# Moving the LayerNorm steps of the last two tiles to other places in the stream, and passing the last LayerNorm between the engines in four pieces

## The reference, cut to what matters

```python
mix = concat([attn, c], axis=-1) @ w_out            # attention and a LayerNormed, SiLUed convolution ("cln")
h = layer_norm(ALPHA * x + mix, ln1_g, ln1_b)       # "ln1"
up = h @ w_up
upc = causal_dwconv(concat([ffn_prev, up]), ffn_dw_w, ffn_dw_b)
f = (silu(upc[..., :2816]) * upc[..., 2816:]) @ w_down
ple = sigmoid(h @ w_pg + b_pg) * (p @ w_pe)
y = layer_norm(ALPHA * h + f + ple, ln2_g, ln2_b)   # "ln2", the output
```

## Time and profile before

| | us |
|---|---|
| median of 3 runs | 2485.96 (2484.69 to 2487.77) |
| the profiled execution, its own time | 2489.22 |
| its span, first to last instruction | 2487.4 |
| PE busy | 2393.0 (96%) |
| POOL busy | 1606.6 (65%) |
| DVE busy | 1449.9 (58%) |
| ACT busy | 1277.6 (51%) |
| mean granted PE clock | 0.982 |

### The profile page before, as it was taken

How to read it: one execution, slowest core, us unless ns; L and a number is a source line. 1 busy time by engine, 2 the same in 40 slices (tenths; PEclk the granted TensorE clock), 3 DMA queues, 4 the chain that set the end, 5 groups by cost and what they waited for, 6 DMA issues and landing times.

```text
span 2487.4 us, 38824 instructions
## 1 busy us (share of the span) xinstructions
PE 2393.0 (96%) x15109; PEld 2351.9 (95%) x15109; DVE 1449.9 (58%) x2338; ACT 1277.6 (51%) x2070; POOL 1606.6 (65%) x1284
## 2 busy tenths in 40 slices
PE   7789999999999999999999999999999999998996
PEld 7789998999999999999999999999899999988996
DVE  5747884467666357666626767652676665264432
ACT  4547555466444446644445654453565435355652
POOL 7447787775665676566567656656865655667773
PEclk9889999999999999999999999999999999999998
DMA  6324454543333444333344433334443332534442
GB/s 226 102 96 153 152 184 152 177 145 117 113 125 115 160 155 144 119 117 127 104 164 155 146 122 115 124 109 162 154 148 109 125 134 97 169 118 165 167 147 79
DMA packets 119046, 341.54 MB, mean 137 GB/s; under 512 B 15312, under 2 KB 43600, under 8 KB 118864
## 3 DMA queue, kind: packets, MB, share of 16 engines
q1 hardware_dynamic: 95408, 311.32, 37.2%
q10 hardware_dynamic: 23456, 27.74, 3.4%
HBM read 330.12 MB, written 8.99 MB: 136 GB/s over the span
## 4 chain that ended last, share of the span: by engine, by line
PE 85%; DVE 6%; ACT 4%; issue 2%; POOL 1%; DMA 1%; ACTq 0%; SPq 0%; DVEq 0%
PE ps L511 27%; PE ps L513 27%; PE ps L512 27%; DVE sq L1116 2%; POOL w_lo L462 1%; PE ps L602 1%; DMA w_raw<-in_panels 1%; ACT w_hi L630 1%; PE ps L550 1%; DVE acc L1053 1%; PE ps L581 1%; PE ps L569 1%; PE ps L559 1%; DVE res L1053 1%; DVE ps L1156 0%
## 5 line engine op out<-in xcount | busy, mean ns | idle before, releaser
L462 POOL TENSOR_TENSOR w_lo<-w_raw,w_hi 128x512 fp32r<-128x512 f32 (+1 forms) x1272 | 1605.6, 1289 | 842.3 <-ACT w_hi L630 840.8
L630 ACT CAST w_hi<-w_raw 128x1024 fp32r<-128x1024 f32 (+1 forms) x636 | 622.2, 981 | 605.9 <-PE ps L513 418.6
L511 PE MATMUL ps<-h_hi,w_hi 128*128 128x386 f32 (+5 forms) x2496 | 816.0, 327 | 9.6 <-DVE f_lo L994 4.1
L512 PE MATMUL ps<-h_lo,w_hi 128*128 128x386 f32 (+5 forms) x2496 | 807.6, 324 | 0.0
L513 PE MATMUL ps<-h_hi,w_lo 128*128 128x386 f32 (+5 forms) x2496 | 807.6, 324 | 0.0
L511 PEld LDWEIGHTS ps<-h_hi,w_hi 128*128 128x128 f32 x2496 | 473.6, 190 | 18.2 <-issue 9.4
L512 PEld LDWEIGHTS ps<-h_lo,w_hi 128*128 128x128 f32 x2496 | 474.3, 190 | 1.3
L513 PEld LDWEIGHTS ps<-h_hi,w_lo 128*128 128x128 f32 x2496 | 474.6, 190 | 0.0
L511 PE MATMUL ps<-f_hi,w_hi 128*128 128x384 f32 (+2 forms) x1264 | 412.0, 326 | 10.1 <-DVE f_lo L994 5.5
L512 PE MATMUL ps<-f_lo,w_hi 128*128 128x384 f32 (+2 forms) x1264 | 407.6, 322 | 0.0
L513 PE MATMUL ps<-f_hi,w_lo 128*128 128x384 f32 (+2 forms) x1264 | 407.5, 322 | 0.0
(11 more groups left out here) (128 smaller groups left out, 2025.2 us busy)
## 6 DMA issues: line engine op xcount, KB each, us to landing
w_raw<-in_panels SPq DMA_DIRECT2D x540, 512.0 KB, 3.2
w_raw<-in_panels SPq DMA_DIRECT2D x48, 384.0 KB, 3.0
w_raw<-in_panels SPq DMA_DIRECT2D x48, 128.0 KB, 2.3
xres<-in_xT ACTq DMA_DIRECT2D x32, 192.0 KB, 2.9
out_yT<-res ACTq DMA_DIRECT2D x4, 1536.0 KB, 6.5
a_raw<-in_xT ACTq DMA_DIRECT2D x6, 768.0 KB, 6.7
out_yT<-res ACTq DMA_DIRECT2D x2, 1024.0 KB, 4.9
x_raw<-in_xT SPq DMA_DIRECT2D x1, 1536.0 KB, 7.3
```

Of the source, the lines that this page charges most:

```text
L462: ins = pool.tensor_tensor(w_lo[:, n % WS, c], w_raw[:, n % RS, c], w_hi[:, n % WS, c].bitcast(F32), ALU.subtract)
L511: pe.matmul(out, w_hi[:, sl, c], hi, start=k == 0, stop=False)
L512: pe.matmul(out, w_hi[:, sl, c], lo, start=False, stop=False)
L630: act.copy(w_hi[:, n % WS, 0:w], w_raw[:, n % RS, 0:w]).then_inc(w_hi_done, 1)
```

## The change

Five things. (1) The cast `h_hi` of ln1 and of cln is a step of its own, `high`. For tiles 1 to 4 it stands one group later (n = 13), with `lo` at 14; for tile 0 one group later too. (2) In tile 4 the steps of ln2 of tile 3 stand later: `tree` 12 (was 11), `mean` and `centre` 15 (13), `square` 16 (14), `sqtree` 18 (16), `var`, `root`, `scale` 20 (18, 18, 19), `affine` 21 as before. (3) ln1 of tile 5 is no longer in `DIRECT`: it gets the two DVE trees, and its steps stand at n = 1, 3, 4, 5, 7. (4) The tree of ln2 of tile 4 stands at n = 7, ahead of the first `u` group, and its other steps at slots 0, 1, 2, 4, 5 (they were at 2, 2, 3, 5, 6, the tree at 0). (5) ln2 of tile 5, the last of the program, gets code of its own: PE adds block m-1 to the mean behind `d` group m, DVE subtracts, ACT squares and DVE scales in four pieces of two blocks each with a semaphore count per piece, the affine is done for blocks 0 to 4 on ACT and 5 to 7 on DVE, and SP sends the output in two halves, four DMAs where ACT sent two.

The core of the diff:

```diff
             one = {2: ("mean", "centre"), 3: ("square",), 6: ("sqtree",), 9: ("var", "root"), 10: ("scale",),
-                   12: ("affine",), 13: ("lo",)}
+                   12: ("affine",), 13: ("high",), 14: ("lo",)}
...
+            if i == LAST - 1:
+                two = {12: ("tree",), 15: ("mean", "centre"), 16: ("square",), 18: ("sqtree",), 20: ("var", "root", "scale"),
+                       21: ("affine",)}
         elif i:
-            one = {0: ("mean", "centre", "square"), 3: ("var", "root", "scale", "affine", "lo")}
-            two = {}
+            one = {1: ("mean", "centre", "square"), 3: ("sqtree",), 4: ("var", "root", "scale"), 5: ("affine", "high"),
+                   7: ("lo",)}
+            two = {7: ("tree",)}
...
-        late = {0: ("tree",), 2: ("mean", "centre", "square"), 3: ("sqtree",), 5: ("var", "root", "scale"), 6: ("affine",)}
+        late = {0: ("mean", "centre"), 1: ("square",), 2: ("sqtree",), 4: ("var", "root", "scale"), 5: ("affine",)}
...
     for m in range(KB):
         stage("d", LAST, 2, m)
-    for name in ("tree", "mean", "centre", "square", "sqtree", "var", "root", "scale", "affine"):
-        stage(name, "ln2", LAST)
+        if m:
+            stage("last_mean", m - 1)
+    stage("last_mean", KB - 1)
+    stage("tree", "ln2", LAST)
+    stage("last_norm")
...
-DIRECT = (("cln", 0), ("ln1", 0), ("ln1", LAST), ("ln2", LAST))
+DIRECT = (("cln", 0), ("ln1", 0))
...
+            y = O["yT"].rearrange("(b p) t -> p b t", p=P)
+            for half in range(2):
+                b = slice(HB * half, HB * half + HB)
+                sp.wait_ge(end_act, LAST_ACT if half else HB)
+                if half:
+                    sp.wait_ge(end_dve, KB - LAST_ACT)
+                for tok, c, cnt in prompt_and_sample(LAST, STARTS[LAST], SEQ):
+                    sp.dma_start(y[:, b, c:c + cnt], res[:, b, tok:tok + cnt]).then_inc(y_out, 16)
...
+            def last_mean(m):
...
+                pe.wait_ge(down_done, (LAST * 3 + 2) * KB + m + 1)
+                mm = pe.matmul(ps[:, AUX, 0:w], mean8[:], res[:, m, 0:w], start=m == 0, stop=m == KB - 1)
...
+            def last_variance():
...
+                for k in range(KB):
+                    if k % 2 == 0:
+                        pe.wait_ge(sq_done, END + k // 2 + 1)
+                    mm = pe.matmul(ps[:, AUX + 1, 0:w], mean8[:], sq[:, k, 0:w], start=k == 0, stop=k == KB - 1)
...
+            def last_norm():
...
+                for n, b in enumerate(PIECES):
+                    act.wait_ge(centred, END + n + 1)
+                    act.activation(sq[:, b, 0:w], res[:, b, 0:w], ACT.Square).then_inc(sq_done, 1)
+                load_functions(ACT.Sqrt)
...
+                for k in range(LAST_ACT):
...
+                    act.wait_ge(scaled, END + k // 2 + 1)
...
+            def last_norm():
...
+                for b in PIECES:
+                    z = res[:, b, 0:w]
+                    dve.tensor_tensor(z, z, std.unsqueeze(1).broadcast_to([P, 2, w]), ALU.mult).then_inc(scaled, 1)
+                dve.wait_ge(scaled, END + len(PIECES))
+                for k in range(LAST_ACT, KB):
+                    r = res[:, k, 0:w]
+                    dve.tensor_scalar(r, r, prm("ln2_g", k), prm("ln2_b", k), ALU.mult, ALU.add).then_inc(end_dve, 1)
```

More of the change, by code:

```diff
@@ L95, in mix_at @@
         for name, n in (("tree", 25), ("mean", 26), ("centre", 26), ("square", 27), ("sqtree", 28), ("var", 29),
-                        ("root", 29), ("scale", 30), ("affine", 31), ("lo", 32)):
+                        ("root", 29), ("scale", 30), ("affine", 31), ("high", 31), ("lo", 32)):
             if k == n:
@@ L137, in plan @@
     stage("conv_add", 0, 3)
-    for name in ("tree", "mean", "centre", "square", "sqtree", "var", "root", "scale", "affine", "lo"):
+    for name in ("tree", "mean", "centre", "square", "sqtree", "var", "root", "scale", "affine", "high", "lo"):
         stage(name, "cln", 0)
@@ L150, in plan @@
             one = {2: ("mean", "centre"), 3: ("square",), 6: ("sqtree",), 9: ("var", "root"), 10: ("scale",),
-                   12: ("affine",), 13: ("lo",)}
+                   12: ("affine",), 13: ("high",), 14: ("lo",)}
             two = {11: ("tree",), 13: ("mean", "centre"), 14: ("square",), 16: ("sqtree",), 18: ("var", "root"),
                    19: ("scale",), 21: ("affine",)}
+            if i == LAST - 1:
+                two = {12: ("tree",), 15: ("mean", "centre"), 16: ("square",), 18: ("sqtree",), 20: ("var", "root", "scale"),
+                       21: ("affine",)}
         elif i:
-            one = {0: ("mean", "centre", "square"), 3: ("var", "root", "scale", "affine", "lo")}
-            two = {}
+            one = {1: ("mean", "centre", "square"), 3: ("sqtree",), 4: ("var", "root", "scale"), 5: ("affine", "high"),
+                   7: ("lo",)}
+            two = {7: ("tree",)}
         else:
-            one = {0: ("mean", "centre", "square"), 2: ("var", "root", "scale"), 4: ("affine",), 5: ("lo",)}
+            one = {0: ("mean", "centre", "square"), 2: ("var", "root", "scale"), 4: ("affine", "high"), 5: ("lo",)}
             two = {}
         if i == 0:
-            one = {0: (0, "var", "root", "scale"), 1: (1, "affine"), 2: (2,), 3: ("lo", 3), 4: (4,)}
+            one = {0: (0, "var", "root", "scale"), 1: (1, "affine"), 2: ("high", 2), 3: ("lo", 3), 4: (4,)}
             for name in ("mean", "centre", "square"):
@@ L218 @@
 NUM = {e: n for n, e in enumerate(ORDER)}
-DIRECT = (("cln", 0), ("ln1", 0), ("ln1", LAST), ("ln2", LAST))
+DIRECT = (("cln", 0), ("ln1", 0))
 LN_NO = {e[1:]: n for n, e in enumerate([e for e in PLAN if e[0] == "tree"])}
+END, LAST_ACT = LN_NO["ln2", LAST], 5
+PIECES = [slice(k, k + 2) for k in range(0, KB, 2)]
 GROUPS = len(ORDER)
 assert len(NUM) == GROUPS == NT * PANELS
-SUM_NO = {e: n for n, e in enumerate([e for e in LN_NO if e not in DIRECT])}
+SUM_NO = {e: n for n, e in enumerate([e for e in LN_NO if e not in DIRECT and e != ("ln2", LAST)])}
 def panel_of(e):
@@ L352, in build @@
                          "probt_done", "o_done", "att_done"))
+    end_act, end_dve = sem("end_act"), sem("end_dve")
     dve_step, act_step = sem("dve_step"), sem("act_step")
@@ L607, in _ @@
                     group(e)
+                elif e[0] == "last_mean":
+                    last_mean(e[1])
+                elif e[0] == "last_norm":
+                    last_variance()
                 elif e[0] == "vt":
@@ L830, in root, with high @@
                 act.activation(ps[:, AUX + 1, 0:w], ps[:, AUX + 1, 0:w], ACT.Sqrt, bias=eps[:, 0:1]).then_inc(std_done, 1)
+            def high(name, t):
+                z, hi, lo, nb, w = ln_of(name, t)
+                act.wait_ge(affine_done, LN_NO[name, t] + 1)
+                act.copy(hi, z).then_inc(hi_done, 1)
             def affine(name, t):
@@ L910, in _ @@
                     affine(*e[1:])
+                elif what == "last_norm":
+                    last_norm()
+                elif what == "high":
+                    high(*e[1:])
         @block.vector
@@ L1123, in sums @@
             def sums(name, t):
-                if (name, t) in DIRECT:
+                if (name, t) in DIRECT or (name, t) == ("ln2", LAST):
                     return
@@ L1164, in rest @@
                 dve.tensor_tensor(lo, z, hi.bitcast(F32), ALU.subtract).then_inc(mix_lo if name == "cln" else h_ready, 1)
+            def last_norm():
+                w = WIDTH[LAST]
+                dve.wait_ge(mean_done, END + 1)
+                for b in PIECES:
+                    z = res[:, b, 0:w]
+                    dve.tensor_tensor(z, z, ps[:, AUX, 0:w].unsqueeze(1).broadcast_to([P, 2, w]), ALU.subtract
+                                      ).then_inc(centred, 1)
+                dve.wait_ge(std_done, END + 1)
+                std = ps[:, AUX + 1, 0:w]
+                own.step(dve.reciprocal(std, std))
+                own.wait()
+                dve.wait_ge(centred, END + len(PIECES))
+                for b in PIECES:
+                    z = res[:, b, 0:w]
+                    dve.tensor_tensor(z, z, std.unsqueeze(1).broadcast_to([P, 2, w]), ALU.mult).then_inc(scaled, 1)
+                dve.wait_ge(scaled, END + len(PIECES))
+                for k in range(LAST_ACT, KB):
+                    r = res[:, k, 0:w]
+                    dve.tensor_scalar(r, r, prm("ln2_g", k), prm("ln2_b", k), ALU.mult, ALU.add).then_inc(end_dve, 1)
             split_x(0)
```

24 lines of the change are left out of this document (16 added, 8 removed).

## The result

| | before | changed |
|---|---|---|
| median of the timed runs | 2486.76 us (2484.69 to 2487.77) | 2460.67 us (2459.88 to 2464.69) |
| ratio | | 0.9906, interval 0.9894 to 0.9918 |
| profiled execution, its span | 2489.22, 2487.4 | 2460.87, 2459.1 |
| mean granted PE clock | 0.982 | 0.986 |

The account below looks back on a forecast made before the run. PE, busy 96% of the span, was taken as the bound, with gains only where it stands still or at the end. 7.7 + 10.4 + 9.7 = 27.8 us off the median 2485.96 gave 2458.2, range 2451 to 2470.

Parts of the forecast that it names:

- part 1: Tile 4: the wait before the mean goes, a wait of 2.1 before `var` stays; 7.7 us gained, bounds 5 and 9.6.
- part 4: Tiles 0 to 3: the moved centring and casts gain 0, with at most 1 us lost in tile 0.
- part 2: Tile 5: shorter ln1 chain and earlier ln2 steps; 10.4 us gained, bounds 6 and 13.3.
- The backlog of 0.8: Tile 5's attention scores lose 0.5 us behind the first SiLU, the transposes 0.3; taken off the gain in tile 4.
- The pause of 4.8: Tile 5: PE, done with `d` 7, stands 4.8 us before `u` 0, where it stood 1.8.
- The walk through the `u` groups: Tile 5: SiLUs and ln2 steps timed in turn; PE idle 0.4 before `u` 14, 2.9 before `u` 16, 2.3 before `d` 0.
- The clock after `d` 0 I leave as it was: Tile 5: the eight `d` groups keep their 28.02 us, against 26.2 at full pace; no gain.
- Part 3: The end: last LayerNorm in pieces, split affine and halved output; 9.7 us gained, bounds 7.1 and 10.5.
- The bound of +2.5 for the low clock: The end: low clock at the last variance would cost 2.5 us, leaving 7.1 gained.
- The middle: Rival, tiles 4 and 5: waits in attention units and ln2 steps take back 14 of 18 us, 2472; chance 0.17.
- The clock: Rival: every new pause of PE is followed by low clock, costing 7.5 us in all, 2465.7; chance 0.14.
- the slower rival: From `u` 0 in tile 4: lag outgrows PE's five banks (21 us), 33 us lost over 22 pairs, 2491; chance 0.04.

Follow-up runs that it names:

- e5: The changed kernel with nearly all of POOL's subtractions left out for the groups around the fills of tiles 4 and 5; 2453.52 us in one run.
- e6: The changed kernel with 14 small matmuls on PE ahead of the variance in tile 4; 2461.08 us in one run.
- e10: The changed kernel with DVE summing blocks 0 to 6 of the last LayerNorm, PE averaging that sum and block 7; 2461.58 us.
- e12: The changed kernel with one piece of eight blocks in the last LayerNorm instead of four pieces of two; 2470.49 us in one run.
- e2: The kernel before with only the steps of ln2 of tile 3 moved in tile 4; 2480.37 us, ratio 0.9980.
- e9: The kernel before with 24 small matmuls on PE ahead of `d` 0 of tile 5; 2486.61 us.
- e1: The kernel before with only the last LayerNorm's new code; 2473.68 us, ratio 0.9959.
- e4: The changed kernel with the cast of the high part back behind the affine in all tiles; 2462.18 us, ratio 0.9906.
- e8: The changed kernel with the high part's cast back and two sums of squares one group earlier; 2460.68 us, ratio 0.9892.

## Why the prediction was right, step by step

The forecast took off 27.8 us. The medians differ by 26.1, and the markers behind the start by 24.9. That is near, but in part by luck: two gains put at nothing (the clock and pace behind `d` 0, 2.3, and the wait for the last addition, 0.8) make up for half of what part 1, part 4 and the rest of part 2 fell short of.

- **Part 1** (7.7; measured 5.8). The mechanism was right: the mean waits no more, `var` does. Its wait was mis-sized, 3.2 and not 2.1: I took `h_lo` at 3.35 and the sum of squares at 5.81, lengths read where POOL happened to collide differently, and missed the product with sin (0.73 and 1.35 for 0.45). `e5` shows that POOL is the cause. The clock was mis-sized too: 2.5 us (6.55 in place of `e6`'s 4.02), where I took 1; in `e10` and `e12` the same code paid nothing. The backlog of 0.8 did not appear (0.03), presumably because PE itself came later; in `e2`, where `u` 0 began 7.4 us earlier, waits of 0.35 and 0.70 stand where I had put 0.5 and 0.3.
- **Part 2** (10.4; measured 0.80 + 6.96 + 2.34 = 10.1). The sum was right by cancelling errors. Before `u` 0: 2.3 forecast, 0.80 found, because the sum of squares took 5.22 and not 3 to 4 (2.66 with POOL quiet). The pause of 4.8 was 4.95. The walk through the `u` groups gave idle of 0.4, 2.9 and 2.3; found were 0, 2.65 and 1.37, the last for `w_lo`. "The clock after `d` 0 I leave as it was" is the step that failed: 2.34 us, some 1.7 by the clock (`e9`, `e1`) and 0.63 by PE's pace. The clock behind `u` 0 cost 1.9, where I took 1.2.
- **Part 3** (9.7; measured 9.66, and 0.75 ahead of it). Each link within 0.1 to 0.4 us: variance begun 1.57 behind the mean (1.5), 4.19 long (4.2), last affine 12.2 behind the mean (12.6). The chain up to the last affine gained 8.7 (8.3), the output 1.0 (1.4). The bound of +2.5 for the low clock was real: with one piece `e12` met it, and with four pieces `e4` met 1.7 of it. The 0.75 ahead is the wait for the last addition, which "in that stretch PE runs without a gap" overlooked. Of the two rules of the Trainium skill weighed there, the drain of the section "What ACT_TABLE_LOAD costs" did not show: the load at 2445.79 takes 1.28, and the next activation starts 1.29 after the load's start. The three `tensor_scalar` blocks took 1.11, between the 0.9 of the rule of "Mode 2×_2P — use both read ports for one tensor" and my 1.4:

```profile
2453.36 1.11 DVE L1243 TENSOR_SCALAR res<-res,par 128x290 f32<-128x290 f32 x3
```

- **Part 4** (0; measured -1.4, and part of part 1's miss). "The sum of squares begins after K in any case" was true; that K's own product could take 1.67 instead of 0.55 was not thought of.
- **The rivals.** The middle did not give its gain back in the changed kernel; it gave back 1.3 of 7.4 in `e2` and 2.5 of 7.6 in `e8`. The clock cost 2.5 in tile 4 and 1.9 in the first two `u` groups of tile 5 (8.46 us at 0.75 for 2 x 3.28), but gave some 1.7 behind `d` 0 and stayed full at the end. The lag for the slower rival never reached five banks.

What stays open: why PE ran the eight `d` groups at two paces with the same granted clock, and what decides the clock behind the pause in tile 4, where the same code gave 0.57, 0.55 and twice 1.00.
